# A causal attention loop on one Trainium2 core: the products with v one step later and in front of the transposes

## The reference, cut to what matters

```
for blk in range(s_len // ATTN_BLOCK):
    s = einsum("bhmqd,bhmkd->bhmqk", q[block], k[:end]) * scale
    s = s - slopes * (tq - tk);  s = where(tk <= tq, s, -inf)
    p = softmax(s, axis=-1)
    a = p[:, :, 0] - lam * p[:, :, 1]
    outs.append(einsum("bhqk,bhkd->bhqd", a, v[:end]))
o = rms_norm(o, attn_sub_norm_g) * (1.0 - lam_init)
```

## Time and profile before

| | us |
|---|---|
| three runs, median (lowest to highest) | 2476.32 (2475.05 to 2476.90) |
| the profiled execution's own time | 2469.51 |
| its span, first to last instruction | 2467.8 |
| scores of block 0 to the last turned rows in MIX | about 301 to 433.1 of the span |
| scores of block 24 to that end (last head and tail) | 389.4 to 433.1 |

### The profile page before, as it was taken

How to read it: one execution, slowest core, us unless ns; L and a number is a source line. 1 busy time by engine, 2 the same in 40 slices (tenths; PEclk the granted TensorE clock), 3 DMA queues, 4 the chain that set the end, 5 groups by cost and what they waited for, 6 DMA issues and landing times.

```text
span 2467.8 us, 30109 instructions
## 1 busy us (share of the span) xinstructions
PE 2261.3 (92%) x11196; PEld 1782.3 (72%) x11196; DVE 1410.8 (57%) x2157; ACT 1127.8 (46%) x1768; POOL 462.7 (19%) x492
## 2 busy tenths in 40 slices
PE   8999697988999984999999997999999999997998
PEld 5777455764777763778877886887777887886886
DVE  4677477326777756367327775355367426775363
ACT  5222377233556644566443444245566453435142
POOL 1047334111233222211220000001211230000000
PEclk9999899999999996999999999999999999999999
DMA  6200110124999876111110003013111110003012
GB/s 200 99 35 1 68 69 1 11 103 160 383 389 381 343 266 223 43 35 35 31 51 17 6 35 137 35 52 104 41 29 35 35 45 22 12 35 137 35 52 94
DMA packets 148397, 239.56 MB, mean 97 GB/s; under 512 B 45232, under 2 KB 101808, under 8 KB 136368
## 3 DMA queue, kind: packets, MB, share of 16 engines
q1 hardware_dynamic: 138304, 221.07, 25.4%
q0 software_dynamic: 8928, 16.80, 1.8%
q10 hardware_dynamic: 1040, 0.00, 0.0%
HBM read 212.13 MB, written 41.42 MB: 103 GB/s over the span
## 4 chain that ended last, share of the span: by engine, by line
PE 49%; DVE 5%; ACT 5%; issue 2%; POOL 1%; DMA 0%; POOLq 0%; ACTq 0%; DVEq 0%
PE ps L105 12%; PE ps L107 12%; PE ps L106 12%; PE ps L95 4%; PE ps L1915 2%; PE ps L1896 1%; PE ps L1897 1%; PE ps L1899 1%; PE ps L1898 1%; PE ps L1900 1%; PE ps L510 1%; DVE sm L2496 1%; PE ps L1792 1%; DVE PTb L2510 1%; DVE xn L2493 1%
## 5 line engine op out<-in xcount | busy, mean ns | idle before, releaser
L106 PE MATMUL ps<-WT_lo,HT_hi 128*128 128x512 f32 x832 | 326.6, 392 | 0.0
L107 PE MATMUL ps<-HT_hi,WF_lo 128*128 128x512 f32 x800 | 314.6, 393 | 0.0
L105 PE MATMUL ps<-HT_hi,WU_hi 128*128 128x512 f32 x704 | 285.2, 405 | 18.7 <-POOL WF_lo L987 6.4
L106 PE MATMUL ps<-H_lo,WU_hi 128*128 128x512 f32 x704 | 276.4, 393 | 0.0
L105 PE MATMUL ps<-W_hi,HT_hi 128*128 128x512 f32 x512 | 202.6, 396 | 8.8 <-DVE MIX_lo L2481 5.9
L107 PE MATMUL ps<-W_hi,MIX_lo 128*128 128x512 f32 x512 | 200.9, 392 | 0.0
L987 POOL TENSOR_TENSOR WF_lo<-WF,WU_hi 128x1024 fp32r<-128x1024 f32 x42 | 110.1, 2621 | 466.5 <-ACT WU_hi L1246 466.5
L106 PEld LDWEIGHTS ps<-WT_lo,HT_hi 128*128 128x128 f32 x832 | 157.9, 190 | 32.1 <-issue 0.5
L107 PEld LDWEIGHTS ps<-HT_hi,WF_lo 128*128 128x128 f32 x800 | 151.8, 190 | 32.5
L1435 ACT ACTIVATE xn<-ps,sm 128x1024 f32<-128x1024 f32 x64 | 71.4, 1116 | 223.8 <-DVE sm L2497 223.8
L105 PEld LDWEIGHTS ps<-HT_hi,WU_hi 128*128 128x128 f32 x704 | 133.7, 190 | 52.5 <-POOL WF_lo L987 8.8
(11 more groups left out here) (449 smaller groups left out, 5528.0 us busy)
## 6 DMA issues: line engine op xcount, KB each, us to landing
WT<-in_w_gate SPq DMA_DIRECT2D x31, 1024.0 KB, 7.4
WT<-in_w_up SPq DMA_DIRECT2D x31, 1024.0 KB, 10.4
MIX<-in_w_down SPq DMA_DIRECT2D x31, 1024.0 KB, 10.5
WF<-in_w_in SPq DMA_DIRECT2D x48, 512.0 KB, 3.8
WT<-in_w_out SPq DMA_DIRECT2D x6, 2048.0 KB, 7.8
H<-in_x SPq DMA_DIRECT2D x16, 512.0 KB, 8.1
h_dram<-H SPq DMA_DIRECT2D x16, 512.0 KB, 2.8
H<-h_dram SPq DMA_DIRECT2D x16, 512.0 KB, 10.5
```

The lines of the kernel that those rows point to most:

```text
L105: pe.matmul(o, lh, rh, start=(i == 0), stop=False)
L106: pe.matmul(o, lh, rl, start=False, stop=False)
L107: mm = pe.matmul(o, ll, rh, start=False, stop=(i == last))
```

## The change

PE makes the products with v of block g-4 at step g, in place of block g-3, and they now stand between the scores and the transposes of the turned weights. The turned rows of block g-6 follow, in place of g-5. ACT's output copy takes block g-4, DVE's copy to MIX block g-6. The three loops run one step longer, and `sm` gets a fifth slot, since a block's statistics now live one step longer. No instruction is added or removed.

```diff
-        sm = sb("sm", [P, 4, 16])
+        sm = sb("sm", [P, 5, 16])
...
-            for g in range(NB + 3):
+            for g in range(NB + 4):
...
-                if g >= 3:
-                    q = g - 3
+                if g >= 4:
+                    q = g - 4
                     act.wait_ge(o_ready, q + 1)
                     if q >= 3:
                         act.wait_ge(ot_ready, q - 2)
-                    act.activation(on[:, q % 3, :], o_bank(q), ACT.Copy, scale=sm[:, q % 4, 6:7])
+                    act.activation(on[:, q % 3, :], o_bank(q), ACT.Copy, scale=sm[:, q % 5, 6:7])
...
-            for g in range(NB + 5):
+            for g in range(NB + 6):
...
+                if 4 <= g < NB + 4:
+                    q = g - 4
+                    h, b = BLOCKS[q]
+                    pe.wait_ge(at_evac, TURNS[q + 1])
+                    if q >= 2:
+                        pe.wait_ge(o_cp, q - 1)
+                    if q >= 3:
+                        pe.wait_ge(ot_evac, q - 2)
+                    accumulate(pe, o_bank(q), [(ATb[:, q % 2, k, :], V1[:, k, h * P:(h + 1) * P]) for k in range(b + 1)]).then_inc(o_ready, 1)
                 if 2 <= g < NB + 2:
                     q = g - 2
                     b = BLOCKS[q][1]
...
-                if 3 <= g < NB + 3:
-                    q = g - 3
-                    h, b = BLOCKS[q]
-                    pe.wait_ge(at_evac, TURNS[q + 1])
-                    if q >= 2:
-                        pe.wait_ge(o_cp, q - 1)
-                    if q >= 3:
-                        pe.wait_ge(ot_evac, q - 2)
-                    accumulate(pe, o_bank(q), [(ATb[:, q % 2, k, :], V1[:, k, h * P:(h + 1) * P]) for k in range(b + 1)]).then_inc(o_ready, 1)
-                if g >= 5:
-                    q = g - 5
+                if g >= 6:
+                    q = g - 6
                     pe.wait_ge(o_n, q + 1)
...
-            for g in range(NB + 5):
+            for g in range(NB + 6):
...
-                if g >= 5:
-                    q = g - 5
+                if g >= 6:
+                    q = g - 6
                     h, b = BLOCKS[q]
                     dve.wait_ge(ot_ready, q + 1)
```

More of the change, by code:

```diff
@@ L909, in _ @@
             for q in range(NB):
-                o, ssq, rsq = on[:, q % 3, :], sm[:, q % 4, 8:9], sm[:, q % 4, 9:10]
+                o, ssq, rsq = on[:, q % 3, :], sm[:, q % 5, 8:9], sm[:, q % 5, 9:10]
                 pool.wait_ge(o_cp, q + 1)
@@ L1151, in _ @@
                         w = sS[m][g % (3 - m)][:, 0:W]
-                        act.activation(w, w, ACT.Exp, scale=-1.0, bias=sm[:, g % 4, m:m + 1], accum_out=sm[:, g % 4, 4 + m:5 + m]).then_inc(e_ready, 1)
-                if g >= 3:
-                    q = g - 3
+                        act.activation(w, w, ACT.Exp, scale=-1.0, bias=sm[:, g % 5, m:m + 1], accum_out=sm[:, g % 5, 4 + m:5 + m]).then_inc(e_ready, 1)
+                if g >= 4:
+                    q = g - 4
                     act.wait_ge(o_ready, q + 1)
@@ L1157, in _ @@
                         act.wait_ge(ot_ready, q - 2)
-                    act.activation(on[:, q % 3, :], o_bank(q), ACT.Copy, scale=sm[:, q % 4, 6:7])
+                    act.activation(on[:, q % 3, :], o_bank(q), ACT.Copy, scale=sm[:, q % 5, 6:7])
                     if q >= 1:
                         act.wait_ge(o_cp, q)
-                    act.activation(osq, o_bank(q), ACT.Square, scale=sm[:, q % 4, 6:7], accum_out=sm[:, q % 4, 8:9]).then_inc(o_cp, 1)
+                    act.activation(osq, o_bank(q), ACT.Square, scale=sm[:, q % 5, 6:7], accum_out=sm[:, q % 5, 8:9]).then_inc(o_cp, 1)
                 if NB - NT <= g < NB:
@@ L2078, in _ @@
                         dve.tensor_tensor_reduce(sS[m][g % (3 - m)][:, 0:W], psf[:, 2 * m * HALF:2 * m * HALF + W], BH[:, S - P - b * P:S],
-                                                 1.0, -NEG, ALU.add, ALU.min, sm[:, g % 4, m:m + 1]).then_inc(s_max, 1)
+                                                 1.0, -NEG, ALU.add, ALU.min, sm[:, g % 5, m:m + 1]).then_inc(s_max, 1)
                 if 1 <= g <= NB:
@@ L2083, in _ @@
                     W = (BLOCKS[q][1] + 1) * P
-                    t = sm[:, q % 4, :]
+                    t = sm[:, q % 5, :]
                     dve.wait_ge(e_ready, 2 * q + 2)
```

## The result

| | before | after |
|---|---|---|
| median of 5 runs | 2476.32 us | 2497.51 us |
| lowest and highest | 2472.92, 2477.01 | 2494.23, 2504.47 |
| ratio to before, 95% interval | | 1.0093 [1.0082, 1.0104] |
| profiled execution: time, span | 2469.5, 2467.8 | 2497.51, 2495.8 |
| mean granted clock of TensorE | 0.972 | 0.962 |

The change costs 21 us, forecast were 7.3. The direction was right and the size was not: 2497.5 lies outside of the range 2476 to 2490. The two profiled executions stand 28 us apart, since that of before lies 6.8 under its median; about 4 of the 28 lie outside the attention, where the two kernels are the same.

The account below looks back on a forecast made before the run. No engine is full; a loop of waits through several engines sets the attention's pace. Last head +6.2, tail +1.3 and heads one to three -0.2 sum to +7.3 us, added to the median: 2483.6 us, range 2476 to 2490.

Parts of the forecast that it names:

- The last head, +6.2: Steps 24 to 30: large products put before the transposes add 7.2 us to the loop, less 1.0 of slack.
- the tail, +1.3: Steps 30 to 37: block 28's products precede block 30's transposes, so the last turned rows in MIX end 1.3 us later.
- the 1.0 us of slack: Last head: ACT's waits for DVE's pass before the exponentials, 1.0 us in all, disappear first and reduce the 7.2 inserted.
- about 0.5 of the inserted 1.8 is hidden: Tail: about 0.5 of 1.8 us inserted is hidden, as block 30's transposes waited for DVE anyway.
- this is covered by that very wait: ACT's output copy, a step later, falls where ACT idles for the transposes, so it costs nothing; uncovered, 0.59 us a step.
- Heads one to three together: -0.2: First three heads: -0.3 at the pipeline's start, -0.7 in the second head, +0.8 in the third, sum -0.2 us.
- third head of 28.0: Head without extra work: a new loop through late exponentials and products takes 28.0 us against 27.18, so +0.8.
- The pointwise steps: Second head: two pointwise steps, costing 5.9 us, get about 0.75 us each covered by room in odd steps, -1.5.
- C: Rival: PE's clock falls in the last head, doubling products and slowing transposes, +8 us, 2492 us; chance 0.07.
- The signs: Expected in the after profile: ACT's largest wait for PE, DVE's score wait falling from 11.5 us, last-head transposes 9.5 to 10 apart.
- A: Rival: early heads gain more than walked, so the two halves nearly cancel, within 5 us, 2480 us; chance 0.29.
- B: Rival: exponentials not held, scores start early in all heads, some 8 of DVE's 11.5 us waiting go, 2468 us; chance 0.06.

Follow-up runs that it names:

- e6: After with turned rows of odd blocks in a bank of their own and extra unread matmuls in last head and tail: 2483.52 us, 1.0039 to before.
- e3: After with turned rows of odd blocks written to bank 5, so they don't wait for another block's output copy: 2493.43 us, 1.0072 to before.
- e4: After with extra unread 128x128 matmuls on PE in the last head's odd steps and in the tail: 2489.15 us, 1.0053 to before.
- e10: After with all eight pieces of w_out made after the loop, out of the last head: 2482.48 us, 1.003 to before.
- e9: Before with all eight pieces of w_out made after the loop, out of the last head: 2470.26 us, 0.9983 to before.
- e8: Before with products with v one step later, behind the transposes, and four buffers for turned weights in place of two: 2477.92 us, 1.0008 to before.
- e5: Before with extra unread matmuls on PE in the tail only: 2472.59 us, 0.9995 to before.

## Why the prediction was wrong in size

**Where the 21 us are.** The three causes, each by a run that takes it away:

| cause | forecast | by the medians | from | in the attention |
|---|---|---|---|---|
| products hold the exponentials | 7.3 | 9.8 | e6 against before | 10.4 |
| turned rows wait for the output copy | 0 | 4.1 to 5.6 | after less e3; e4 less e6 | 7.8; 3.8 |
| clock in last head and tail | 0 (rival, 8) | 8.4 to 9.9 | after less e4; e3 less e6 | 9.9; 5.9 |

The last column is read from the traces, from the first scores of block 0 to the start of the last row in MIX: 139.8 us in before, 163.9 in after, 156.1 in e3, 154.1 in e4 and 150.2 in e6. Taken away one after the other, clock first, the parts are 9.9, 3.8 and 10.4 of 24.1 us. Taken away in the other order they are 7.8, 5.9 and 10.4: about 4 us belong to both causes, as freeing the turned rows also moves the first fall of the last head two pairs later. The medians, with intervals of some 3 us each, agree with these parts.

**The last head, +6.2, and the tail, +1.3: the mechanism and nearly the size.** With the clock held (e4), last head and tail together cost 51.32 - 43.34 = 8.0 us, and the forecast was 7.5. It was split otherwise: 4.8 and 3.2. The term of the last head was some too large (more was hidden than the 1.0 us of slack), and that of the tail too small. The step that failed in the tail is "about 0.5 of the inserted 1.8 is hidden". In e4's tail:

```profile
438.19 1.58 PE L95 MATMUL ps<-WF,HT 128*128 128x128 f32 x12 [1.89 <-ACT xn L1161]
```

These are the products of block 28. They wait for ACT's output copy (3.72 us in after). DVE had finished the combination that the transposes of block 30 need at 437.77, before these products start, so all of their time is on the path. Those transposes start 8.41 us after the scores of block 31, against 5.33 in before, which is 3.1 of the 3.2 us. The pieces of w_out don't make this: without them the same comparison, e10 less e9, gives 14.83 - 11.98 = 2.9.

**The step that failed most: "this is covered by that very wait".** I asked only what the later output copy costs ACT, and found it covered by ACT's wait for the transposes. I didn't ask who waits for the copy. PE does, at the turned rows of the next lines of its own program, and in the odd steps it had been the large products that covered this. With the copy behind exponentials that I had myself forecast to be 1.86 us late, the wait follows from the same walk. "Heads one to three together: -0.2" became +6.3 on the ruler (first head 0.65, second 2.48, third 3.16), and +1.1 with the turned rows freed (e6: -0.06, -0.11, +1.27). My third head of 28.0 is nearly met by 28.45 there. The pointwise steps gave back what I said: in e6 the second head is 4.55 us longer than the third, in before 5.92, so 1.4 for the 1.5; the second head comes to -0.1 in place of -0.7 because the head under them grew by 1.3 for 0.8, which is the miss of the third head again. Up to 1 us of the second head of after is clock: right behind a wait of 1.63 us in front of the turned rows the scores of block 14 took 2.35 us in place of 1.35, and the like in e4 and e10, which have the same heads, but not in e3 and e6. So in the table it stands with the turned rows.

**The clock: the right rival with the wrong chance.** C was priced at +8 on top of the forecast, and the measured price is 8.4 (e4). That the two agree is partly luck: C priced doubled products and transposes in the last head alone, while 5.5 of the 9.9 us in the traces lie in the tail, and in the last head scores were slow as well, but not all products (those of block 22 took 1.38 us, at full speed). It had 0.07, because I had only two rows and took from them that the clock holds at PE busy 2.89 of 4 us and falls only in nearly empty stretches. In after it fell with PE busy 6.97 of 10. The reason for the low chance was the sentence "the traces so far bear the fall out only for emptier stretches"; that is a statement on what had been seen, and I used it as a bound. Forecast and C together were worked out, as 2492 us, and the range was stopped at 2490, below them. With the missed wait of the turned rows, 4.1 to 5.6, on top of 2492 they come to what was measured.

**The signs.** The late exponentials (4.89 us behind the scores, 4.90 by the walk), ACT's wait as the largest, and the low part's 3 us came as said. DVE's wait for scores rose instead of falling, in part by the missed term, since the turned rows kept the scores; but with them freed it still is 11.7 us in 13 waits (e3), as large as before, so this sign fails by itself. The third head (30.3 for 27.5 to 28.5) and 61.6 us from block 24 to the end for 51 were out. The transposes of blocks 24, 26 and 28 start at 411.20, 423.76 and 434.63, so 12.6 and 10.9 us apart, where 9.5 to 10 was said. With the clock held (e4) they start at 410.57, 420.66 and 430.33, 10.09 and 9.67 apart, which is what was said within 0.1.

**Rivals A and B.** The gain they spoke of exists. It is 0.8 us in the third head and 1.0 in the second (e8), under the condition that B named, that ACT's wait ends before DVE's first pass of the step does: at step 20 of e8 it ends at 376.38, the pass at 376.76. B's price, 8 of the 11.5 us, was far too high: over three heads e8 wins 2.7 (first 0.9, second 1.0, third 0.8).

## What to carry to other kernels

When a block of work is moved out of a step, list the waits that it covered there, not only the work that it delayed: here one transposition of 0.3 us that waits for another engine's copy came into the open and cost 4.1 to 5.6 us. Put nothing between the operation that starts a chain through several engines and the first link of that chain, neither by program order nor by a shared buffer; with four buffers the same delay was 24.6 us cheaper. And when an edit lengthens a stretch in which PE already waits, work out the time at half clock on top of the forecast and let the range reach to it, unless rows of such a stretch show that the clock holds; two rows of emptier stretches didn't show that.

## What the runs showed of the hardware that I had not expected

**The clock falls in the middle of busy work.** In after the granted clock is 0.83 over stretches of 10 us with PE busy 6.6 to 7.8 of them, and the scores that stand on the path run at half speed: 3.29 and 2.93 us in place of 1.77 and 1.56. With the 12 extra matmuls an odd step, PE busy 8.6 to 9.1 in the last head, it stays 1.00. But the busy share of such a stretch doesn't decide by itself. In e3 the clock was 1.00 from 400 to 420 with PE busy less than in after:

```profile
400.00:410.00 10.00, 6.16 (x41) 4.26 (x41) 6.89 (x19) 7.21 (x21) 3.57 (x8) 1.00 0.01 2
410.00:420.00 10.00, 6.06 (x41) 4.25 (x41) 6.82 (x20) 6.41 (x19) 3.04 (x8) 1.00 0.00 0
```

(Time at half clock counts as busy, so the two can't be compared directly either: 6.97 at 0.83 is less work than it looks.) What exactly lets it fall in one and not in the other stays open; the runs show that it stays at 1.00 in the last head with more matmuls (e4) and without the pieces of w_out (e10).

**A fall can cost nothing.** In e5, whose last head has the code of before, the large products of step 29 took 2.93 us in place of 1.80 (the clock is 0.83 from 410 to 420), and the head took the same 28.86 us: the scores of block 30 started 0.4 us later than in before, counted from those of block 29, and those of block 31 were on time again (8.09 us after block 29's, 8.10 in before). So the same code can show the fall in one execution and not in another, and where the operations behind have slack for it, it has no price.

**The fall seems to feed itself.** In after the clock falls in each pair of steps from block 26 on and comes back, each time on the scores or the products that the other engines wait for. The large scores follow each other after 9.3, 10.8 and 12.5 us in after, after 9.3, 9.6 and 10.0 in e3, where the clock holds up to block 30, and after 10.1, 9.3 and 10.0 in e4. That a slow stretch lengthens the next gap and so brings the next fall is my reading of these rows; no run takes the gap apart from the fall. A head whose pairs get longer towards its end, with the same work, is a sign to look at the clock.
